# Thirteen boundaries that turn the token tiles into features one block at a time, and gate sums laid out chunk by chunk

## The reference

```python
# between two dense parts (first block; the others use an RMS norm, some without shift and scale)
x = layer_norm(DN_ALPHA * x + res_w * (1.0 + gate) * y, g, b)
h = x * (1.0 + scale) + shift            # per feature
y = swiglu(h, w_in, w_out)               # or retention, attention, ...

# expert layer of the second block, over 128-token blocks
act = gelu(einsum('td,ted->te', h, u[experts]))
out = einsum('te,ted->td', gates * act, v[experts])
```

## Time and profile before

| | us |
|---|---|
| median of 3 runs | 3756.14 |
| lowest and highest | 3748.13, 3759.78 |
| the profiled execution | 3750.75 |
| its span, first to last instruction | 3748.9 |

### The profile page before, as it was taken

How to read it: one execution, slowest core, us unless ns; L and a number is a source line. 1 busy time by engine, 2 the same in 40 slices (tenths; PEclk the granted TensorE clock), 3 DMA queues, 4 the chain that set the end, 5 groups by cost and what they waited for, 6 DMA issues and landing times. The chain is left out here.

```text
span 3748.9 us, 59725 instructions
## 1 busy us (share of the span) xinstructions
PE 3605.2 (96%) x22322; PEld 3085.1 (82%) x22322; DVE 3024.6 (81%) x6306; ACT 2046.6 (55%) x4309; POOL 133.9 (4%) x132
## 2 busy tenths in 40 slices
PE   6999999999899979999999999999999999999998
PEld 5887688888788758998888887899988888887787
DVE  7887688887688776988989966689798997798866
ACT  3554455655455545645656456554566554556555
POOL 0000000000000001400000000050000000000000
PEclk9999999999889989999999999999999999999999
DMA  8767376776257514445555454244555445586454
GB/s 328 274 257 281 112 292 242 275 256 242 106 218 270 202 68 151 176 158 180 180 180 180 167 188 175 95 176 159 174 177 184 177 176 179 218 303 269 151 189 156
DMA packets 119617, 744.51 MB, mean 199 GB/s; under 512 B 13857, under 2 KB 14273, under 8 KB 44833
## 3 DMA queue, kind: packets, MB, share of 16 engines
q1 hardware_dynamic: 118082, 737.57, 53.9%
q10 hardware_dynamic: 416, 2.07, 0.1%
q0 software_dynamic: 832, 1.06, 0.1%
HBM read 738.54 MB, written 1.05 MB: 197 GB/s over the span
## 5 line engine op out<-in xcount | busy, mean ns | idle before, releaser
L226 PE MATMUL bank<-h_split,weights_high 128*128 128x512 f32 (+1 forms) x5824 | 1712.8, 358 | 14.1 <-DVE h_split L744 7.9
L1137 ACT ACTIVATE weights_high<-weight_ring 128x512 fp32r<-128x512 f32 x2248 | 1292.4, 624 | 633.9 <-PE bank L226 375.2
L1145 DVE TENSOR_TENSOR weights_low<-weight_ring,weights_high 128x512 fp32r<-128x512 f32 x2168 | 1396.2, 688 | 274.9 <-ACT weights_high L1137 252.9
L226 PE MATMUL bank<-h_split,weights_low 128*128 128x256 f32 x4800 | 1267.7, 280 | 0.0
L226 PEld LDWEIGHTS bank<-h_split,weights_high 128*128 128x128 f32 x5824 | 1013.4, 189 | 161.0 <-issue 14.0
L226 PEld LDWEIGHTS bank<-h_split,weights_low 128*128 128x128 f32 x4800 | 909.7, 190 | 38.2 <-issue 0.8
L226 PE MATMUL acc<-weights_high,hidden_high 128*128 128x512 f32 x1552 | 613.3, 395 | 2.5 <-DVE hidden_low L1319 2.3
L226 PE MATMUL acc<-weights_low,hidden_high 128*128 128x512 f32 x1552 | 604.9, 390 | 0.0
L226 PE MATMUL acc<-weights_high,hidden_low 128*128 128x512 f32 x1552 | 604.7, 390 | 0.0
L226 PEld LDWEIGHTS acc<-weights_high,hidden_low 128*128 128x128 f32 x1552 | 291.3, 188 | 63.3
L226 PEld LDWEIGHTS acc<-weights_low,hidden_high 128*128 128x128 f32 x1552 | 291.6, 188 | 59.6 <-issue 0.2
(11 more groups left out here) (352 smaller groups left out, 3433.4 us busy)
## 6 DMA issues: line engine op xcount, KB each, us to landing
weight_ring<-stream SPq DMA_DIRECT2D x574, 1024.0 KB, 4.8
h_feat<-slots SPq DMA_DIRECT2D x96, 512.0 KB, 5.9
h_tok<-slots SPq DMA_DIRECT2D x94, 512.0 KB, 5.9
work<-slots SPq DMA_DIRECT2D x26, 512.0 KB, 8.4
mod_sums<-biases SPq DMA_DIRECT2D x7, 1536.0 KB
h_feat<-rows SPq DMA_DIRECT2D x8, 512.0 KB, 3.8
work<-rows SPq DMA_DIRECT2D x7, 512.0 KB, 4.7
work<-biases SPq DMA_DIRECT2D x1, 1536.0 KB
```

Of the source, the lines that this page charges most:

```text
L226: ins = self.nc.tensor.matmul(out, lhs, rhs, start=start, stop=stop)
L1137: act.activation(k.w_hi[:, b, q * self.QUARTER:(q + 1) * self.QUARTER], self.raw(g, q), ACT.Copy).then_inc(k.highs_ready, 1)
L1145: return eng.tensor_tensor(k.w_lo[:, b, w], self.raw(g, q), k.w_hi[:, b, w].bitcast(F32), ALU.subtract)
```

## The change

It makes four edits.

1. **Single blocks on VectorE.** `place_by_vector` handles one block at a time with one two-operation instruction (times scale, plus shift) in place of one four-block multiply and one four-block add.
2. **Another division of the blocks.** Half 0 of tile 1 is placed by VectorE instead of ScalarE, and of half 1 of tile 1 ScalarE places two blocks and VectorE the other two. VectorE waits for ScalarE's two blocks before its own.
3. **The first gate product ahead of the transposes.** In the eight boundaries with gate products, the first stands between the one-column sums and the transposes, and the second stays behind them.
4. **Gate sums chunk by chunk.** `whole` and `second` are stored with the token as the inner index, so line 2306 reads them without a step; the copy and the add read their bank with a step instead.

```diff
+            if not self.gate_later:
+                self.wait_accumulated(pe)
+                self.gate_row(pe, 0)
...
         if self.sums is not None and not self.gate_later:
-            for h in range(2):
-                mm = self.gate_row(pe, h)
-            mm.then_inc(k.banks_for_scalar.sem, k.banks_for_scalar.send())
+            self.gate_row(pe, 1).then_inc(k.banks_for_scalar.sem, k.banks_for_scalar.send())
...
+    def wait_accumulated(self, pe):
+
+        k = self.k
+        if self.gated:
+            pe.wait_ge(k.acc_read.sem, self.read + 1)
+        else:
+            pe.wait_ge(k.tiles_added.sem, self.added + 1)
...
+    BY_VECTOR = ((1, 0), (0, 1), (1, 1))
+    PARTS = ((0, 0), (1, 1))
+    BY_SCALAR = ((0, 0), (1, 0), (0, 1), (1, 1))
+
+    def fill_by_vector(self, dve):
+
+        self.place_by_vector(dve, 1, 0, range(4))
+        self.place_by_vector(dve, 0, 1, range(4))
         self.low(dve, 0, 0)
-        self.place_by_vector(dve, 1)
         self.low(dve, 0, 1)
-        for t in range(TT):
-            self.low(dve, 1, t)
-
-    def place_by_scalar(self, act, t):
+        dve.wait_ge(self.k.scalar_placed.sem, self.scalar_placed + len(self.PARTS))
+        self.place_by_vector(dve, 1, 1, range(2, 4))
+        self.low(dve, 1, 0)
+        self.low(dve, 1, 1)
+
+    def fill_by_scalar(self, act):
+
+        self.place_by_scalar(act, 0, 0, range(4))
+        self.high(act, 0, 0)
+        self.high(act, 1, 0)
+        self.high(act, 0, 1)
+        self.place_by_scalar(act, 1, 1, range(2))
+        self.high(act, 1, 1)
+
+    def place_by_scalar(self, act, half, t, chunks):
...
-        act.wait_ge(k.feature_banks.sem, self.banks + 2 * t + 1)
-        for c in range(4):
+        act.wait_ge(k.feature_banks.sem, self.banks + 2 * t + half + 1)
+        for c in chunks:
+            c = 4 * half + c
...
+        sem, n = k.scalar_placed.sem, self.scalar_placed + self.PARTS.index((half, t)) + 1
+        ins.then_inc(sem, 1)
+        act.wait_ge(sem, n)
...
+    def place_by_vector(self, dve, half, t, chunks):
 
...
-        dst, shape = self.part_of(k.h_t, 1, t), [P, 4, P]
-        scale = (a if self.sums is not None else self.columns(0))[:, 4:8]
-        dve.wait_ge(k.feature_banks.sem, self.banks + 2 * t + 2)
-        ins = dve.tensor_tensor(dst, k.bank[:, 2 * t + 1, :].rearrange("p (c t) -> p c t", t=P),
-                                scale.unsqueeze(2).to_broadcast(shape), ALU.mult)
-        if self.sums is not None:
-            ins.then_inc(k.dve_step, 1)
-            dve.wait_ge(k.dve_step, k.step("dve"))
-            ins = dve.tensor_tensor(dst, dst, b[:, 4:8].unsqueeze(2).to_broadcast(shape), ALU.add)
+        dve.wait_ge(k.feature_banks.sem, self.banks + 2 * t + half + 1)
+        for c in chunks:
+            c = 4 * half + c
+            dst = k.h_t[:, c, t * P:(t + 1) * P]
+            if self.sums is not None:
+                ins = dve.tensor_scalar(dst, self.turned(c, t), a[:, c:c + 1], b[:, c:c + 1], ALU.mult, ALU.add)
+            else:
+                ins = dve.tensor_scalar(dst, self.turned(c, t), self.columns(0)[:, c:c + 1], None, ALU.mult)
         ins.then_inc(k.placed.sem, 1)
 
+    def wait_placed(self, eng, half, t):
+        if (half, t) in self.BY_VECTOR:
+            eng.wait_ge(self.k.placed.sem, self.placed + self.BY_VECTOR.index((half, t)) + 1)
...
     def low(self, dve, half, t):
         k = self.k
-        if half == 1:
-            dve.wait_ge(k.placed.sem, self.placed + t + 1)
-        dve.wait_ge(k.input_highs.sem, self.inputs + TT * half + t + 1)
+        self.wait_placed(dve, half, t)
+        dve.wait_ge(k.input_highs.sem, self.inputs + self.BY_SCALAR.index((half, t)) + 1)
...
-                           k.bank[:, bank, :].rearrange("p (t i n) -> p i t n", t=n, i=PIECES)[:, 1],
+            act.activation(self.second[:, :, t:t + n],
...
-                pieces = k.bank[:, bank, :].rearrange("p (t i n) -> p i t n", t=n, i=PIECES)
+                pieces = k.bank[:, bank, :].rearrange("p (t i n) -> p i n t", t=n, i=PIECES)
...
-                dve.tensor_tensor(self.whole[:, t:t + n, :], pieces[:, 0], self.second[:, t:t + n, :],
+                dve.tensor_tensor(self.whole[:, :, t:t + n], pieces[:, 0], self.second[:, :, t:t + n],
                                   ALU.add).then_inc(k.gated, units)
...
-            gates = self.whole.rearrange("p t n -> p n t")
+            gates = self.whole
...
-    whole, second = room(BATCH, QUARTER), room(BATCH, QUARTER)
+    whole, second = room(QUARTER, BATCH), room(QUARTER, BATCH)
```

More of the change, by code:

```diff
@@ L181, in __init__ @@
         self.normed = Count(ctx, nc, "tiles_normed")
+        self.scalar_placed = Count(ctx, nc, "placed_by_scalar")
         self.feature_banks = Count(ctx, nc, "feature_banks")
@@ L558, in __init__ @@
         self.banks = k.feature_banks.reserve(2 * TT)
-        self.placed = k.placed.reserve(TT)
+        self.placed = k.placed.reserve(len(self.BY_VECTOR))
+        self.scalar_placed = k.scalar_placed.reserve(len(self.PARTS))
         if update is not None:
@@ L795, in scalar @@
             act.wait_ge(k.vector_for_scalar.sem, k.vector_for_scalar.take())
-        for t in range(TT):
-            self.place_by_scalar(act, t)
-            self.high(act, 0, t)
-        for t in range(TT):
-            self.high(act, 1, t)
+        self.fill_by_scalar(act)
         if self.sums is not None and not self.gate_later:
@@ L987, in vector @@
             self.rescale(dve, t)
-        self.place_by_vector(dve, 0)
-        self.low(dve, 0, 0)
-        self.place_by_vector(dve, 1)
-        self.low(dve, 0, 1)
-        for t in range(TT):
-            self.low(dve, 1, t)
+        self.fill_by_vector(dve)
     def square_again(self, act, t):
@@ L2241, in take_seconds @@
                 act.wait_ge(k.gated, self.fills[self.batch_before(q, b, 1)][i][5])
-            act.activation(self.second[:, t:t + n, :],
-                           k.bank[:, bank, :].rearrange("p (t i n) -> p i t n", t=n, i=PIECES)[:, 1],
+            act.activation(self.second[:, :, t:t + n],
+                           k.bank[:, bank, :].rearrange("p (t i n) -> p i n t", t=n, i=PIECES)[:, 1],
                            ACT.Copy).then_inc(k.seconds_out, 1)
```

7 lines of the change are left out of this document (2 added, 5 removed).

## The result

| | before | changed kernel |
|---|---|---|
| median us (runs) | 3755.07 (14) | 3761.52 (14) |
| lowest and highest | 3748.13, 3759.92 | 3752.26, 3766.51 |
| the profiled execution, its span | 3750.75, 3748.9 | 3766.51, 3764.7 |

The ratio is 1.0019, with a 95% interval of 1.0011 to 1.0026. The change makes the kernel some 7 us slower. That is less than the 0.3% of which the prediction spoke, but the interval leaves out 1.0000. The profiled execution of the changed kernel is the slowest of its fourteen, so its span overstates the loss.

A forecast was written before the change was run, and what follows sets the result against it. TensorE, busy 96% of the span, was taken as the bound, with boundaries paced by VectorE and ScalarE. Dear blocks gave +3.1 us, cheap ones -6.8; the middle, -1.9, from 3756.1 gave 3754 us, range 3744 to 3764.

The forecast's parts named there:

- relay and late gate product: Rival at the boundaries: dear blocks plus slower handovers between engines give 3763 us; chance 0.15, a third beyond 0.3%.
- dearer handovers: Between engines, 0.15 us each rather than 0.05, three more in each of 13 boundaries: 3.9 us.
- The price of a block: One 128-column block placed by VectorE from a bank: 401 ns with shift, 342 without.
- dear blocks: VectorE's blocks at 401 and 342 ns: boundaries +0.75 us, gate product +2.3, in all +3.1 us.
- cheap ones: VectorE's blocks with free operands and half the fixed part overlapped, 0.85 us for four: in all -6.8 us.
- The relay: Boundary's second half: ScalarE's two blocks, VectorE's two, high, low; TensorE reaches block 4 0.2 us later in seven boundaries.
- The gate product: Ahead of the transposes: hidden at some boundaries, on the path at 853, 1075, 3232 and 3549 us; +2.3 us net.
- the 1.3 us that I had coming back: Less gate work queued behind the transposes starts the first product sooner: 0.9 us at 3232 us, 0.4 at 462.
- The rival of the clock: In eight gated boundaries the gate product keeps TensorE's clock up, 4 us on top of cheap blocks: 3745 us; chance 0.12.
- The layout: Expert quarters, gate sums chunk by chunk: 27.8 us less of VectorE, but TensorE has no gap, so 0 us.
- the 28 that I had named as a sign: Expert quarters: VectorE's busy time 28 us lower in all, with the stretches as long as before.
- SyncE's queue: First load behind a boundary waits for a last low 0.75 us later; 22 us of products ahead, so 0.

The follow-up runs named there:

- single_blocks: The kernel before with only VectorE's one-instruction blocks, in the old division and order: 3750.23 us beside 3752.31, ratio 0.9996.
- blocks_only: The kernel before with single blocks on VectorE and the new division, gate products and expert layout as they were: 3755.60 us beside 3752.31, ratio 1.0008.
- no_gate_move: The changed kernel with both gate products behind the transposes: 3753.82 us beside 3751.13, ratio 1.0016, and 1.0005 without one execution of 3794.54 us.
- gate_move_again: The kernel before with only the first gate product ahead of the transposes in all eight boundaries, a repeated run: 3762.08 us beside 3752.95, ratio 1.0024.

## Why the prediction was wrong

The forecast was a small gain (3754 us from 3756.14), and the kernel lost 7. The median of 3761.52 lies inside the range. The rival on the other side, relay and late gate product, is what happened, to which I gave 0.15. That its 3763 us lies so near is in part luck: it got there by 3.9 us for dearer handovers, which no run priced one by one, on top of a relay and a gate product that were both too cheap, and without the layout's gain.

**The price of a block** was right to the nanosecond (402 and 342 ns). The step that failed is the last one: having worked out +3.1 us with dear blocks, I took the middle towards cheap ones, -1.9, with the reason that an operand's fetch may be hidden in a row of narrow instructions. Nothing in the rows spoke for this, and the rows had given the dear price by two independent differences. The dear end alone (+3.1) would have had the sign, though less than half of the size. The estimate that I had worked out from the Trainium skill's table, 258 ns for a block (page "VectorE: DVE Perf Modes", section "The TRN2 errata — SBUF-src ops pay a fixed extra latency per instruction"), is 144 ns under the measurement. Its rule that narrow tiles pay the fixed part each time, which it gives for sources in local memory, holds here for sources in a bank: two blocks take 0.73 us, and one instruction on a tile of four times the width 0.69. But the total was no slower, as *single_blocks* shows.

**The relay** was seen, but its stall was mis-sized: +0.2 us predicted for a boundary, 0.61 less some 0.05 measured. The 1.66 us from first product to block 4 was read at 237 us, where the first product still ran at the lower clock (0.64 us). Elsewhere it is 1.48. And the last low ends 8.3 us behind the first transpose in *blocks_only*, where I had 8.13 (245.45 less 237.32). The boundaries without shift, which I had at -0.05 each, have the stall too, 0.31 us. Over twelve boundaries the traces give +5.8 us, where I had +0.75 for all. The ratios give less: about +3 us for both block edits (1.0008), which is not clear of noise, and +4.5 for the division alone (1.0008 against 0.9996).

**The gate product** was mis-sized too: +2.3 us predicted, +5.2 by the traces in its eight boundaries, +6.8 to +9.8 by the four ratios (1.0018 to 1.0026). I had read its cover off one execution, place by place: free at 237, 462, 658 and 3431 us. It cost most at 3431, and 0.9 at 3549 us, where I had 1.6. The other executions show that the cover of 1.6 us hangs on where the clock falls, and in half of the cases it falls within the sums. Then the sums take up the cover, and the product itself takes 2.05 us instead of 1.1. In the kernel before, that lottery is hidden in the boundaries up to 1075 us, since nothing but the sums stands in the gap. Of the 1.3 us that I had coming back, some 0.5 did at 3232 us; the 0.4 at 462 us was peculiar to the one trace that I had read, which has 15.06 us there against 14.6 in the three others without an edit of the order. The 2 to 4 us between traces and ratios stay open: the four traces are mostly of quick executions (spans 3752.3, 3753.1, 3754.1 and 3762.6, where the medians less what lies around the span are 3758 to 3760).

**The rival of the clock** happened in part, and was worth little. In the boundary near 237 us the granted clock is 0.89 in the changed kernel and was 0.53, and the sixteen transposes last 2.66 us instead of 4.08. Yet ScalarE places 1.16 us behind the first transpose instead of 1.21. I had priced this at 0.5 us. At the first product it was worth 0.3 us there (5.97 us behind the first transpose, 6.26 in *no_gate_move*) and 0.06 to 0.26 in the seven others, which the late transposes outweigh. My reason against it, that the fall begins with the idle time ahead of the sums, doesn't hold either: in the trace of the kernel before the granted clock is 1.00 in each microsecond up to 236, when the sums are nearly done.

**The layout** was costed at 0 on TensorE's 359.89 busy us of 360. It gained 1.0 us in each layer, of 27.3 us taken from VectorE's busy time, and 0.1% by the ratio. (In the changed kernel VectorE's busy time fell by 16.4 us and not by the 28 that I had named as a sign: the blocks that it took over added some 10, as *blocks_only* shows with 3034.7 us against 3024.6.) The failed step is the reading of that row: eight waits of 0.2 us, and smaller ones, lie within what counts as busy. The durations were right (692 ns where I expected 686; the add stayed at 416).

**SyncE's queue** was right: a wait of 1.2 us more, and no change in the stretches between boundaries that follows it.

## What to carry to other kernels

Work moved into a gap needs the gap's length in the worst execution, not in the one that was profiled: here one-column products filled 3.7 or 5.3 us of it depending on the clock, and a product of 1.1 or 2.05 us fitted in only half the time. Where bounds of a cost are derived and one of them rests on read rows and the other on a hope, take the first as it is. Where a handover chain gets longer, compare its end with the time that the consumer takes to reach it at full clock, since a reading at the lower clock flatters the slack.

## What the runs showed of the hardware

- Where TensorE's clock falls in a boundary differs between executions of one kernel: at 237 us the one-column sums took 3.73 us in one and 5.28 in another. The Trainium skill says so of the start of a kernel ("it's run-variable", page "TensorE: Matmul & The Clock Gate", section "Part 1: The HAM clock gate"); here it holds in the middle of one.
- Within the 35 executions of the kernel before that stood beside *gate_move_again*, an execution with a mean granted clock lower by 0.001 took 2.2 us longer (correlation -0.69). That is about half of the variance between 3748 and 3760 us. The mean clock of *gate_move_again* is the same as that of before, 0.9759, so its 9 us don't show as more time at the lower clock.
- A narrow VectorE instruction out of the accumulator memory with two per-partition operands repeats every 0.32 us (eight in 2.64 us, the last 0.40), though each lasts 0.40.
- A step of 32 elements in a read out of local memory costs VectorE 428 ns for 512 elements (1,120 against 692). Out of the bank the same step costs nothing that shows (684 to 686 ns), and a step of 64 costs the add nothing (416 ns before and after) and ScalarE's copy 3 ns (377 against 374).
